# Opening of the second FFN: order of products, operands, squares and their sums

## What is computed

```python
xp = xp + mp[2] * op
xs = xs + ms[2] * os_
hp = rmsnorm(xp, g_ffn_norm[i]) * (1 + mp[4]) + mp[3]
hs = rmsnorm(xs, g_ffn_norm[i]) * (1 + ms[4]) + ms[3]
xp = xp + mp[5] * swiglu(hp, w_ffn_gate[i], w_ffn_up[i], w_ffn_down[i])
xs = xs + ms[5] * swiglu(hs, w_ffn_gate[i], w_ffn_up[i], w_ffn_down[i])

def adaln(cond, w, b):
    m = jax.nn.silu(cond) @ w + b
    return [t[..., None, :] for t in jnp.split(m, 6, axis=-1)]

def swiglu(h, wg, wu, wd):
    return (jax.nn.silu(h @ wg) * (h @ wu)) @ wd
```

## Time and profile before

| | us |
|---|---|
| median of 3 runs | 1657.77 |
| lowest and highest | 1656.53, 1658.71 |
| the profiled execution | 1658.6 |
| its span, first to last instruction | 1656.5 |

### The profile page before, as it was taken

The page is one execution under the profiler, slowest core; times in us unless marked ns, Lnnn a source line. Parts: engine busy times, 40 slices in busy tenths (PEclk is TensorE's granted clock), DMA queues, the critical chain, the costliest instruction groups (busy, mean ns, idle before and its releaser), DMA issues.

```text
span 1656.5 us, 28354 instructions
## 1 busy us (share of the span) xinstructions
PE 1612.9 (97%) x10988; PEld 1515.3 (91%) x10988; DVE 1174.0 (71%) x2033; ACT 844.9 (51%) x1462; POOL 97.4 (6%) x147
## 2 busy tenths in 40 slices
PE   6999999999999999999999999998999999999997
PEld 4878788799899999999989999998889999999997
DVE  5546465679857758767767887787898588586775
ACT  4634425356524425334547777786575254252443
POOL 1211110200100000000000000000000000000000
PEclk9999999999999999999999999999999999999998
DMA  9554354532433423332322222223122232222312
GB/s 322 163 164 139 118 183 131 174 116 68 134 105 102 121 83 87 115 93 93 108 67 76 66 76 64 64 60 120 58 77 73 81 102 70 77 84 65 102 41 88
DMA packets 230393, 171.06 MB, mean 103 GB/s; under 512 B 10643, under 2 KB 210998, under 8 KB 230262
## 3 DMA queue, kind: packets, MB, share of 16 engines
q1 hardware_dynamic: 216182, 120.37, 25.1%
q0 software_dynamic: 14080, 48.90, 8.6%
HBM read 160.32 MB, written 4.72 MB: 100 GB/s over the span
## 4 chain that ended last, share of the span: by engine, by line
PE 90%; DVE 5%; ACT 2%; issue 2%; DMA 1%; SPq 0%; DVEq 0%; POOL 0%; ACTq 0%; POOLq 0%
PE acc L834 45%; PE acc L1216 25%; PE side L1216 4%; PE side L1395 2%; PE side L1440 1%; PE acc L1440 1%; PE work L1369 1%; PE side L869 1%; PE work L869 1%; PE side L1056 1%; DVE x L2670 0%; PE acc L1038 0%; PE work L1395 0%; PE acc L869 0%; PE acc L1090 0%
## 5 line engine op out<-in xcount | busy, mean ns | idle before, releaser
L834 PE MATMUL acc<-h_hi,w_hi 128*128 128x320 f32 x1006 | 243.0, 323 | 6.2 <-DVE h_lo L2361 2.0
L834 PE MATMUL acc<-h_lo,w_hi 128*128 128x320 f32 x1006 | 231.2, 311 | 0.0
L834 PE MATMUL acc<-h_hi,w_lo 128*128 128x320 f32 x1006 | 230.1, 310 | 0.0
L834 PEld LDWEIGHTS acc<-h_hi,w_hi 128*128 128x128 f32 x1006 | 165.6, 190 | 32.3 <-issue 21.0
L2670 DVE SCALAR_TENSOR_TENSOR x<-acc,mods,x 128x320 f32<-128x320 f32 (+2 forms) x249 | 94.1, 434 | 124.2 <-PE acc L834 123.9
L834 PEld LDWEIGHTS acc<-h_lo,w_hi 128*128 128x128 f32 x1006 | 170.4, 190 | 0.0
L1216 PE MATMUL acc<-ax_hi,ff_hi 128*128 128x322 f32 x528 | 166.1, 315 | 4.2 <-issue 2.7
L834 PEld LDWEIGHTS acc<-h_hi,w_lo 128*128 128x128 f32 x1006 | 170.2, 190 | 0.0
L1216 PE MATMUL acc<-h_hi,w_hi 128*128 128x322 f32 x616 | 167.1, 313 | 2.6 <-issue 1.6
L1216 PE MATMUL acc<-ax_hi,ff_lo 128*128 128x322 f32 x528 | 164.7, 312 | 0.0
L1216 PE MATMUL acc<-ax_lo,ff_hi 128*128 128x322 f32 x528 | 164.7, 312 | 0.0
(11 more groups left out here) (462 smaller groups left out, 3567.2 us busy)
## 6 DMA issues: line engine op xcount, KB each, us to landing
a_raw<-in_w_ada_dram POOLq DMA_DIRECT2D x80, 512.0 KB, 6.2
ff_raw<-in_w_ffn_gate_dram SPq DMA_DIRECT2D x88, 256.0 KB, 3.4
ff_raw<-in_w_ffn_up_dram SPq DMA_DIRECT2D x88, 256.0 KB, 4.3
w_raw<-in_w_gla_in_dram SPq DMA_DIRECT2D x24, 512.0 KB, 3.9
ff_raw<-in_w_ffn_down_dram SPq DMA_DIRECT2D x32, 384.0 KB, 3.5
w_raw<-in_w_diff_qkv_dram SPq DMA_DIRECT2D x24, 512.0 KB, 4.0
ff_raw<-in_w_ffn_down_dram SPq DMA_DIRECT2D x32, 320.0 KB, 3.2
a_left<-in_w_ada_dram SPq DMA_DIRECT2D x8, 512.0 KB, 9.6
```

The source lines that it names most:

```text
L834: mm = pe.matmul(out[:, s, 0:HALF + s * more], w[:, k * P:(k + 1) * P], a(k)[:, s * HALF:(s + 1) * HALF + s * more], start=(k == 0 and n = ...
```

## The change

On TensorE the last adaLN block moves out of the gemm of unit 6 and stands behind P1 and P7 of the second FFN's tile 0. The three parts of the square sums, until now between pieces of P6 and P2, are made together: in the first FFN in front of P5, in the second behind P5. On ScalarE, in the second layer, operands and scalings are put in front of squares, the scaling of x tile 6 follows square 0, the P1 weights of tile 1 stand in front of the scaling of x tile 7, and the copy of P6 to u2_t stands in front of the high parts of P4's and P3's weights instead of behind them and the table load. On VectorE, in the second layer, x tile 6 is updated before the first two squares are added, and additions of squares stand behind operands. `last_operands` serves only the first layer, with its order unchanged.

```diff
                     if p == 0:
+                        if layer == 1:
+                            ada_block(ADA_LAST)
                         product(layer, 0, "P6", 0, JT - 1)
                         pe.wait_ge(acc_free[1], FFN[layer])
                         product(layer, 1, "P1")
                         if layer == 0:
                             pe.wait_ge(ada_mod, ADA_TAIL + 1)
                         product(layer, 0, "P2", 0, JT - 1)
-                        sum_squares(n, 0, 2)
                         product(layer, 0, "P6", JT - 1)
                         product(layer, 0, "P2", JT - 1)
-                        sum_squares(n, 2, 3)
+                        if layer == 0:
+                            sum_squares(n)
                         product(layer, 0, "P5")
+                        if layer == 1:
+                            sum_squares(n)
                         product(layer, 0, "P4")
...
-            gemm(DIF_OUT + 4, 0, KD, h_hi_k, h_lo_k, {3: [lambda: ada_block(ADA_LAST)]})
+            gemm(DIF_OUT + 4, 0, KD, h_hi_k, h_lo_k)
...
             def ffn_begin(layer, n, m):
 
+                if layer == 1:
+                    kept(layer, 0, "P6")
                 weight_hi(layer, 0, "P4")
                 weight_hi(layer, 0, "P3")
                 act.activation(small[:, 56:57], ones[:, 0:1], ACT.Ln)
-                kept(layer, 0, "P6")
+                if layer == 0:
+                    kept(layer, 0, "P6")
...
                 scaled_x(3, 5, x_updated(5))
                 square(0)
+                scaled_x(3, 6, x_updated(6))
+                operand_hi(1, "s2", 0)
                 square(1)
+                operand_hi(1, "s2", 1)
                 square(2)
-                operand_hi(1, "s2", 0)
+                operand_hi(1, "h1", 0)
+                operand_hi(1, "h2", 0)
+                operand_hi(1, "s2", 2)
+                kept(1, 0, "P1")
+                weight_hi(1, 1, "P1")
+                operand_hi(1, "h1", 1)
+                operand_hi(1, "h2", 1)
+                scaled_x(3, 7, x_updated(7))
+                operand_hi(1, "h1", 2)
+                operand_hi(1, "h2", 2)
                 square(3)
+                weight_hi(1, 0, "P5")
+                operand_hi(1, "s2", 3)
+                operand_hi(1, "h1", 3)
                 square(4)
-                operand_hi(1, "s2", 1)
+                operand_hi(1, "h2", 3)
                 square(5)
-                last_operands(1, 3, x_updated)
+                kept(1, 0, "P7")
+                square(6)
+                square(7)
...
                 operands(1, 2)
                 operands(1, 3)
-                add_squares(3, 1)
-                add_squares(3, 2)
                 sixth()
                 operands(1, 4)
+                add_squares(3, 1)
+                operands(1, 5)
+                add_squares(3, 2)
+                operand_sums(1, 6)
+                operand_lo(1, "h1", 0)
+                operand_lo(1, "h2", 0)
+                operand_lo(1, "s2", 2)
+                add_to_x(*out_unit(9), KD - 1, 8)
+                weight_lo(1, 1, "P1")
+                operand_lo(1, "h1", 1)
+                operand_lo(1, "h2", 1)
+                operand_lo(1, "h1", 2)
+                operand_sums(1, 7)
+                operand_lo(1, "h2", 2)
                 add_squares(3, 3)
-                operands(1, 5)
+                weight_lo(1, 0, "P5")
+                operand_lo(1, "s2", 3)
+                operand_lo(1, "h1", 3)
                 add_squares(3, 4)
-                last_operands(1, lambda: add_to_x(*out_unit(9), KD - 1, 8), lambda: add_squares(3, 5))
+                operand_lo(1, "h2", 3)
+                add_squares(3, 5)
```

More of the change, by code:

```diff
@@ L1893, in projection, with last_operands @@
                 operand_hi(0, "s2", 1)
-                last_operands(0, n, updated)
-            def last_operands(layer, n, updated):
+                last_operands(n, updated)
+            def last_operands(n, updated):
                 scaled_x(n, 6, updated(6))
[L1899 to L1906, removed]
+                operand_hi(0, "h1", 0)
+                operand_hi(0, "h2", 0)
+                operand_hi(0, "s2", 2)
+                operand_hi(0, "h1", 1)
+                operand_hi(0, "h2", 1)
                 squares(n, 6, lambda: act.wait_ge(*updated(6)))
-                operand_hi(layer, "h1", 2)
-                operand_hi(layer, "h2", 2)
+                operand_hi(0, "h1", 2)
+                operand_hi(0, "h2", 2)
                 scaled_x(n, 7, updated(7))
[L1911 to L1917, removed]
+                kept(0, 0, "P1")
+                weight_hi(0, 1, "P1")
+                weight_hi(0, 0, "P5")
+                operand_hi(0, "s2", 3)
+                operand_hi(0, "h1", 3)
+                operand_hi(0, "h2", 3)
                 squares(n, 7, lambda: act.wait_ge(*updated(7)))
-                kept(layer, 0, "P7")
+                kept(0, 0, "P7")
             def kept(layer, i, name):
@@ L2767, in down_lo, with last_operands @@
                     .then_inc(lo_ready, 1)
-            def last_operands(layer, add_six, add_seven):
+            def last_operands(add_six, add_seven):
                 add_six()
[L2772 to L2779, removed]
-                add_seven()
[L2781 to L2789, removed]
+                operand_sums(0, 6)
+                operand_lo(0, "h1", 0)
+                operand_lo(0, "h2", 0)
+                operand_lo(0, "s2", 2)
+                operand_lo(0, "h1", 1)
+                operand_lo(0, "h2", 1)
+                add_seven()
+                operand_lo(0, "h1", 2)
+                operand_lo(0, "h2", 2)
+                weight_lo(0, 1, "P1")
+                operand_sums(0, 7)
+                weight_lo(0, 0, "P5")
+                operand_lo(0, "s2", 3)
+                operand_lo(0, "h1", 3)
+                operand_lo(0, "h2", 3)
             def projection(first, l, n, beside):
@@ L2833, in sixth @@
                     add_squares(n, 5)
-                last_operands(0, sixth, lambda: add(7))
+                last_operands(sixth, lambda: add(7))
             def c11(layer, i):
```

## The result

The changed kernel takes 1660.13 us (median of 20 runs, 1657.86 to 1661.71), the kernel before 1656.68 us in the 20 runs beside it (1655.06 to 1658.71). The ratio is 1.0019, with a 95% interval from 1.0013 to 1.0024: slower by 0.19%, 2.2 to 4.0 us. The profiled execution took 1661.19 us, its span is 1659.1 us (before 1656.5).

What follows compares the result with a forecast made beforehand. The time at which VectorE takes the variance was taken to set the end. Terms +0.7, +1.4, +0.8 and -0.1 gave +2.8, with rounding +2.9, so a median of 1660.7 us; range 1657.3 to 1662.6 us.

Steps and rivals of the forecast that it cites:

- What bounds the opening: Second FFN's opening: the end follows when VectorE takes the variance, through the third tile's scaling that TensorE awaits 1.47 us.
- The adaLN block: Its 16 products, 1.95 us with the seam, leave the gemm and fill TensorE's idle time behind P7, 1196.5 to 1198.5.
- Operands in front of squares: ScalarE and VectorE, second FFN: s2 up to 3 us earlier, but TensorE pauses 2.9 us before P6's last piece.
- P5 in front of the sums: Second FFN: the variance would wait 0.7 us for sums ending at 1215.3; +0.7 us without a fall of the clock.
- The clock: After pauses of 2.9 and 3.1 us it falls: P5 slow, +1.4 us, and part of the sums slow, +0.8 us.
- The first FFN: The sums move behind the last pieces of P6 and P2, nothing stalls, one seam goes: -0.1 us, between 0 and -0.4.
- A longer low clock: First rival: the lower level covers P5 and most sums, variance at 1218.6, +3.8 us, 1661.6 us; chance 0.25.
- No fall: Second rival: the clock stays up or the pauses are shorter, +0.7-0.1 us, 1658.4 us; chance 0.17.
- Faster: Third rival: the copy to u2_t ends before 1209.6, variance 0.35 us earlier, -0.5 us, 1657.3 us; chance 0.08.
- the walk: Three engine queues stepped through in the new order with profiled durations, trusted to some tenths; TensorE resumes 3.0 us later.

Runs made afterwards that it cites:

- clock kept: Changed kernel with the adaLN block's 16 products computed again in each of TensorE's two pauses; ratio 1.0007 to the kernel before, 1657.96 us.
- scaling put forward: Changed kernel with VectorE's scaling of P3 of the second FFN's third tile five operations earlier in its queue; ratio 1.0019 to the kernel before, 1660.05 us.
- adaLN block alone: Kernel before with only the last adaLN block moved out of the gemm to behind P7 of the second FFN; ratio 1.0006, 1658.03 us.
- sums in front of P5: Changed kernel with the second FFN's square sums made before P5 instead of behind it; ratio 1.0004 to the kernel before, 1657.82 us.
- the block moved, no fillers: Changed kernel with adaLN block before P6's last piece, second FFN's sums before P5, ScalarE's P4 and P3 splits earlier; ratio 1.0001 to the kernel before, 1656.27 us.

## Why the prediction was right, point by point

- **What bounds the opening.** "The end follows the time at which VectorE takes the variance" held to 0.03 us. From the variance to the final sum of squares it is 428.78 to 428.81 us in all nine profiles whose order behind the variance is the kernel before's, with the variance anywhere between 34.34 and 39.72 us. That it passes through the one scaling at 1252 didn't hold: taken away, it gave 0.48 us and not 1.4, since VectorE's next tile is nearly as late. By this the carrier is VectorE's queue as a whole; no run takes out every wait for it.
- **The adaLN block.** It was costed at nothing won, and alone it moves the variance by 0.01 us. What it does is to fill a pause; with the operands in front P6 then started at 1198.46 (1198.5 worked out).
- **Operands in front of squares.** s2 of piece 3 was worked out for 1206.2 and ended at 1206.25, P6's last piece for 1206.3 and came at 1206.30, the copy to u2_t for 1210.3 and ended at 1210.34, P5 for 1210.35 and came at 1210.44. The pauses were given as 2.9 and 3.1 us and are 2.76 and 2.70: the last pieces between them take 1.4 us to their end, not 0.9 (the second row comes 0.25 us behind the first, the second piece 0.34 us behind the first one's last row, and the last row is 0.31 us long); it changed nothing behind.
- **P5 in front of the sums.** +0.7 worked out, 0.81 measured with the clock kept.
- **The clock.** +1.4 and +0.8 worked out, 1.50 and 0.75 by the rows and 2.21 at the variance, the largest term. That the size fits so well is in part luck: the low stretch ended in the first part of the sums here and later in the profile with the scaling put forward. And a long pause alone doesn't bring the fall, as the reading of 2.50 and 1.57 us suggests: behind 2.76 us P6's last piece ran at full clock. One of the 20 executions took 1657.86 us at a mean clock of 0.994, the others 1658.3 to 1661.7 us at 0.990 to 0.992; that would fit an execution without the fall, but it wasn't profiled. The rule of the Trainium skill (TensorE: Matmul & The Clock Gate, "HAM oscillation — how this bites in real kernels"), short bursts with waits between them start cold, is told there of a kernel with waits of 3 to 5 us, longer than these. It agrees with P5's rows, 0.47 us long, and not with P6's last piece, whose rows were 0.31 us long behind 2.76 us of wait.
- **The first FFN.** -0.1 worked out; its variance came 0.02 us earlier and the next product 0.06 later: nothing, since VectorE waits 0.21 us for the sums there now.
- **The rivals.** A longer low clock (+3.8) showed in the profile with the scaling put forward, whose opening is the changed kernel's: the variance is at +3.45 us instead of +3.02. No fall (+0.6) was seen in the profiles only with 32 products more. Faster did not come by itself: the copy to u2_t ended at 1210.34, 0.7 us behind the point given.
- **The level.** Forecast was 1660.7, from a median of three runs of 1657.77 plus 2.9; the time is 1660.13, and 20 runs of the kernel before have 1656.68. The move is +3.45 in medians, +3.0 by the distances in the profiles. So the starting point was 1.1 us too high and the move 0.55 too small, and that the time came within 0.6 us of the forecast is in part luck. What the walk got right is the move by the distances, +3.0 for +2.9; the 0.4 us up to the medians' move aren't explained.

## What to carry to other kernels

Look for the operation from which the distance to the end is the same in every version, and cost an edit by what it does to that operation; here 1.9 us of TensorE work moved into a pause won nothing, and a wait of TensorE far behind was mostly a copy: taken away, 1.46 us of it gave 0.48. When work that covered a wait is moved away, cost the pause that stays and what the clock does to the rows behind it: filling 2.7 us pauses with repeated products won back 2.2 us of the change's 3.0. Where the operands of a sum are made later, the sum's place has to move with them, and in front of the long product, not behind it.

## What the runs showed of the hardware

- Two pauses of 2.76 and 2.70 us with 1.4 us of work between them were followed by the lower level for nearly 7 us (0.60, 0.50 and 0.53 of full in the three stretches from 1208 to 1215.4), through P5, though products ran without a break from 1210.44 on. With 0.90 and 0.84 us of pause left the clock stayed at 1.00.
- The length of one pause doesn't tell the fall. Within two rows the clock was low behind single pauses of 2.50 us (the kernel before), 2.69 us (adaLN block alone) and 2.74 us (scaling put forward), and the rows behind 2.76 us (changed kernel) and 2.75 us (sums in front of P5) ran at full clock. Behind 1.57 us there was none in the kernel before, behind 0.89 and 1.50 us with 1.4 us of work between them there was one (the block moved, no fillers).
- The length of the low stretch differs too: 3.4 us behind the pause of 2.50 us and 6.5 us behind that of 2.69 us, products running in both; and with the order of the changed kernel the variance is 39.22 or 39.65 us behind the same row.
- At the lower clock a row of products is 0.47 us long instead of 0.31, and a part of the FP32 sums is 2.50 us long instead of 1.24.
